# Retention in a two-block transformer kernel: weight sums by adding transfers, sums of x through PSUM, and one operation for normalising and gating

## The reference, cut to what matters

```
q, k, v, g = split(h @ w_in)              # h = rmsnorm(x); w_in is 1024 x 6144
q, k = rope(q), rope(k) * 256 ** -0.5
...                                       # state and decay in chunks of 64
o = o_intra + o_cross                     # (512, 4 heads, 512)
mu, var = mean(o), mean((o - mu) ** 2)    # over the 512 of a head
o = (o - mu) * rsqrt(var + EPS) * gn_g
y = silu(g) * o
x = x + y @ w_out
```

## Time and profile before

| | us |
|---|---|
| median of 3 runs | 1906.8 (1903.63 to 1907.77) |
| profiled execution, device time | 1903.31 |
| its span in the trace | 1901.5 |
| mean granted clock of TensorE | 0.988 of full |
| TensorE busy | 1830.7 |
| VectorE, ScalarE, GpSimd busy | 1262.2, 874.0, 1018.6 |
| retention, from the spread of the first norm to the end of head 3 | about 545 to 985 |

### The profile page before, as it was taken

One profiled execution on the slowest core, in us unless ns is written; L12 is line 12 of the kernel. 1 busy time (PEld: TensorE's weight loads), 2 busy tenths in 40 slices (PEclk: granted clock), 3 DMA queues, 4 the chain that ended last, 5 costly groups with the idle time before them and its releaser, 6 DMA issues.

```text
span 1901.5 us, 23957 instructions
## 1 busy us (share of the span) xinstructions
PE 1830.7 (96%) x9348; PEld 1557.2 (82%) x9348; DVE 1262.2 (66%) x1908; ACT 874.0 (46%) x1350; POOL 1018.6 (54%) x431
## 2 busy tenths in 40 slices
PE   9999999999977999999899999999999999999998
PEld 7778889898865787878689898988888887888886
DVE  6986875776779667575766354457777766454546
ACT  5345443343543424243446444454666655453444
POOL 5573465475535365656438475665333335664755
PEclk9999999999997999999999999999999999999999
DMA  5222414423245325151342422312433223414221
GB/s 183 89 89 77 145 67 148 159 92 106 80 147 183 133 71 187 66 171 67 110 145 77 133 89 89 134 45 66 121 109 101 88 69 109 155 47 149 92 90 55
DMA packets 143344, 206.02 MB, mean 108 GB/s; under 512 B 4320, under 2 KB 94704, under 8 KB 142720
## 3 DMA queue, kind: packets, MB, share of 16 engines
q1 hardware_dynamic: 135968, 192.16, 30.2%
q10 hardware_dynamic: 7264, 12.34, 2.2%
HBM read 193.96 MB, written 10.53 MB: 108 GB/s over the span
## 4 chain that ended last, share of the span: by engine, by line
PE 72%; DVE 15%; ACT 4%; issue 3%; POOL 1%; DMA 0%; ACTq 0%; DVEq 0%
PE ps L858 23%; PE ps L860 23%; PE ps L859 23%; DVE ps L2315 1%; POOL w_lo L824 1%; ACT w_hi L1411 1%; DVE w_lo L2563 1%; DVE work L2611 1%; DVE raw L2549 1%; DVE diagonals L1983 1%; DVE work L2778 1%; DVE work L2574 0%; DVE probs_t_lo L2797 0%; PE ps L1198 0%; DVE x L2627 0%
## 5 line engine op out<-in xcount | busy, mean ns | idle before, releaser
L824 POOL TENSOR_TENSOR w_lo<-raw,w_hi 128x1024 fp32r<-128x1024 f32 x216 | 527.4, 2451 | 609.4 <-ACT w_hi L1411 609.4
L858 PE MATMUL ps<-xh,w_hi 128*128 128x512 f32 x1280 | 504.9, 394 | 4.6 <-DVE xl L2009 2.3
L860 PE MATMUL ps<-xh,w_lo 128*128 128x512 f32 x1280 | 498.9, 390 | 0.0
L859 PE MATMUL ps<-xl,w_hi 128*128 128x512 f32 x1280 | 498.8, 390 | 0.0
L1411 ACT ACTIVATE w_hi<-raw 128x1024 fp32r<-128x1024 f32 x242 | 252.2, 1057 | 392.9 <-PE ps L860 344.2
L858 PEld LDWEIGHTS ps<-xh,w_hi 128*128 128x128 f32 x1280 | 240.7, 188 | 58.5 <-issue 8.9
L859 PEld LDWEIGHTS ps<-xl,w_hi 128*128 128x128 f32 x1280 | 240.8, 188 | 50.7 <-issue 1.9
L860 PEld LDWEIGHTS ps<-xh,w_lo 128*128 128x128 f32 x1280 | 240.7, 188 | 50.7
L858 PE MATMUL ps<-hid,w_hi 128*128 128x256 f32 (+1 forms) x688 | 228.4, 332 | 2.1 <-DVE att_v L2751 1.1
L860 PE MATMUL ps<-hid,w_lo 128*128 128x256 f32 (+1 forms) x688 | 227.1, 330 | 0.0
L859 PE MATMUL ps<-hid,w_hi 128*128 128x256 f32 (+1 forms) x688 | 227.0, 330 | 0.0
(11 more groups left out here) (302 smaller groups left out, 3546.7 us busy)
## 6 DMA issues: line engine op xcount, KB each, us to landing
raw<-in_mlp_w_dram SPq DMA_DIRECT2D x40, 1024.0 KB, 5.5
work<-in_mlp_w_dram SPq DMA_DIRECT2D x16, 1024.0 KB, 5.5
raw<-in_ret_w_in_dram SPq DMA_DIRECT2D x12, 1024.0 KB, 5.2
raw<-in_att_w_in_dram SPq DMA_DIRECT2D x12, 1024.0 KB, 5.3
raw<-in_w_gate_dram SPq DMA_DIRECT2D x11, 1024.0 KB, 5.4
raw<-in_w_up_dram SPq DMA_DIRECT2D x11, 1024.0 KB, 5.5
hid<-position_sums SPq DMA_DIRECT2D x10, 1024.0 KB, 5.2
raw<-in_w_in_dram SPq DMA_DIRECT2D x9, 1024.0 KB, 5.1
```

The source lines that it names most:

```text
L824: nc.gpsimd.tensor_tensor(half_of(wl[:, b % 2, :], b, half), half_of(source, b, half), half_of(wh[:, b % 2, :], b, half).bitcast(F32), ALU ...
L858: nc.tensor.matmul(o, a[0], b[0], start=first, stop=False, skip_group_check=True)
L859: nc.tensor.matmul(o, a[0], b[1], start=False, stop=False, skip_group_check=True)
L860: return nc.tensor.matmul(o, a[1], b[0], start=False, stop=last, skip_group_check=True)
```

## The change

- `d2` and `d4` leave `BY_VECTOR`: GpSimd makes their low halves too.
- The four sums of quarters are made by transfers that add into the holder. GpSimd issues them: `b12` gets `b11` added (behind the `k` block, for `d1`), then `b22` (behind `d1`'s low halves, for `d2`), then `b21` (behind `d2`'s, for `d4`); `b22` gets `b12` added (behind `h22`'s low halves, for `d3`). Differences become sums, with signs moved to the sums of x and to `value_sum`. Each of the 16 transfers moves 1 MB.
- The order in which SyncE fetches changes; `h22`'s sum of x stays in SBUF and is no longer stored and fetched; the stores have a semaphore each.
- Sums of x: a first sum `w` is built in PSUM, the others from it, with ScalarE scaling tiles into PSUM; all five steps stand before the diagonals, the last two behind `rope` of the queries.
- TensorE in head 0: `h11` ahead of `spread`, scores behind `h22`. Last head: the mix of tiles 2 and 3 behind `h21`, as in the other heads.
- `refine_root` in four operations instead of five, its first value in PSUM. `normalised` goes: ScalarE scales the gates by the root's inverse (`scale_gate`), and `gated` subtracts the mean and multiplies in one operation.
- `scale_x` moves: tiles 0 to 3 ahead of `gate_sum`, tiles 4 to 7 ahead of the output sums.

The diff, cut to its core:

```
-BY_VECTOR = ("t2", "t4", "d2", "d4")
+BY_VECTOR = ("t2", "t4")
...
+            def add_to(held, name, h, signal):
+                dst = holders[holder_of(held, h)].rearrange("p (k c) -> p k c", c=512)
+                nc.gpsimd.dma_start(dst, head_weights(name, h), accum_op=ALU.add).then_inc(signal, 16)
...
-                if kind == "h11":
...
-                    for cut in (slice(0, 1024), slice(1024, 2048)):
-                        nc.gpsimd.tensor_tensor(first[:, cut], second[:, cut], first[:, cut], ALU.subtract).then_inc(d1_made, 1)
+                if kind == "own" and own_at[b][0] == "k":
+                    h = own_at[b][1]
+                    pool.wait_ge(*landed("b12", h))
+                    add_to("b12", "b11", h, p1_landed)
+                if kind == "d1":
                     pool.wait_ge(w_lo, lows[2 * b + 2])
+                    add_to("b12", "b22", head_of(b), p2_landed)
                 if kind == "h22":
...
+                    pool.wait_ge(w_lo, lows[2 * b + 2])
+                    add_to("b22", "b12", head_of(b), p3_landed)
+                if kind == "d2":
+                    pool.wait_ge(w_lo, lows[2 * b + 2])
+                    add_to("b12", "b21", head_of(b), p4_landed)
...
+                    def scale_gate(h):
+                        act.wait_ge(root_refined, h + 2)
+                        for s in range(ST):
+                            act.wait_ge(gate_made, 4 * h + s + 1)
+                            nc.scalar.activation(sg[:, s, :], sg[:, s, :], ACT.Copy, scale=t4[:, s:s + 1]).then_inc(gate_scaled, c.made(gate_scaled))
...
                     for h in range(RET_HEADS):
                         head_quarter("h11", h)
-                        head_scores()
-                        for kind in ("d1", "h22", "d2", "d3"):
-                            head_quarter(kind, h)
+                        if h == 0:
+                            spread()
+                        else:
+                            head_scores()
+                        head_quarter("d1", h)
+                        head_quarter("h22", h)
+                        if h == 0:
+                            head_scores()
+                        head_quarter("d2", h)
+                        head_quarter("d3", h)
...
                     def gated(i):
-                        dve.wait_ge(gate_made, c.next(gate_made))
-                        dve.wait_ge(dve_step, c.now(dve_step))
-                        V.tensor_tensor(o_sb[:, i, :], o_sb[:, i, :], sg[:, i, :], ALU.mult).then_inc(p_ready, c.made(p_ready))
+                        dve.wait_ge(gate_scaled, c.next(gate_scaled))
+                        V.scalar_tensor_tensor(o_sb[:, i, :], o_sb[:, i, :], mv[:, i, 0:1], sg[:, i, :],
+                                               ALU.subtract, ALU.mult).then_inc(p_ready, c.made(p_ready))
...
-                        second_difference(h)
-                        difference_lo("d2", h)
-                        fourth_difference(h)
-                        if h == 0:
-                            scale_x(range(0, 4))
...
+                        if h == 0:
+                            scale_x(range(0, 4))
+                        gate_sum(0)
+                        gate_sum(1)
+                        mixed_stats()
+                        gate_copy(0)
+                        refine_root()
+                        gate_copy(1)
+                        for i in range(ST):
+                            gated(i)
...
-                    position_sum(0)
-                    position_sum(1)
-                    position_sum_lo(0)
-                    position_sum_lo(1)
+                    for kind in ("w", "d2", "d1"):
+                        position_sum(kind)
+                    position_sum_lo("d1")
+                    position_sum_lo("d2")
                     rope(qh, ql, 0)
+                    position_sum("h22")
+                    position_sum_lo("h22")
+                    position_sum("d3")
+                    position_sum_lo("d3")
                     V.tensor_copy(ms, r1c).then_inc(to_curve, c.made(to_curve))
                     refine_root()
                     diagonals(rc2, spread=False)
-                    position_sum(2)
-                    position_sum(3)
-                    position_sum_lo(2)
-                    position_sum_lo(3)
                     rope(kh, kl, 2, take_r1=True)
```

More of the change, by code:

```diff
@@ L393, in build @@
         sum_lo = sem("sum_lo")
-        sums_stored = sem("sums_stored")
+        sum_stored = [sem(f"sum_stored{i}") for i in range(4)]
         sum_landed = [sem(f"sum_landed{i}") for i in range(3)]
@@ L480, in head_source @@
                 return holders[holder_of(*own_at[b])]
-            return holders[roles[head_of(b)][{"h11": 0, "d1": 0, "h22": 2, "d2": 0, "d3": 1, "h21": 3, "d4": 0}[plan[b]]]]
+            return holders[roles[head_of(b)][{"h11": 2, "d1": 0, "h22": 1, "d2": 0, "d3": 1, "h21": 3, "d4": 0}[plan[b]]]]
         def first_turn(f):
@@ L618, in _ @@
                     sp.wait_ge(unit_done, 2 * (begins("ffn") + 30))
[L619 removed]
                     fetch("b12", 0)
+                    fetch("b22", 0)
                     for h in range(RET_HEADS):
@@ L1202, in _ @@
                     first_units(order, double=True)
-                    spread()
                     for h in range(RET_HEADS):
@@ L2502, in refine_root @@
-                        V.tensor_tensor(rc2, rc2, ms2, ALU.mult).then_inc(dve_step, c.made(dve_step))
-                        dve.wait_ge(dve_step, c.now(dve_step))
-                    def position_sum(n):
-                        u, s1, s2, s3 = (by_tile(sum_rows[m]) for m in (2, 0, 1, 2))
-                        s4 = by_tile(sum_rows[3])
-                        if n == 0:
+                        V.scalar_tensor_tensor(rc2, ms2, 1.5, root_guess, ALU.add, ALU.mult).then_inc(root_refined, c.made(root_refined))
@@ L2510, in position_sum @@
+                    def position_sum(kind):
+                        near, far, held = slice(0, 256), slice(256, 512), by_tile(ps[:, 6:8, :])
+                        if kind == "w":
                             dve.wait_ge(scaled_x, 4)
+                        elif kind == "d3":
+                            dve.wait_ge(scaled_x, 8)
                         else:
                             dve.wait_ge(sum_made, c.now(sum_made))
+                        k0, cut, op = {"w": (0, near, ALU.add), "d2": (0, far, ALU.subtract), "d1": (0, near, ALU.add),
+                                       "h22": (4, near, ALU.add), "d3": (0, near, ALU.subtract)}[kind]
+                        made = held if kind == "w" else by_tile(sum_rows[SUM_ROW[kind]])
@@ L2513, in position_sum @@
                         for k in range(4):
-                            g, g_beyond = prow("mix_norm_g_2", k), prow("mix_norm_g_2", 4 + k)
-                            near, far = (slice(0, 256), slice(256, 512))
-                            out_, in_, scale, op, other = ((s1, x[:, 4 + k, far], g_beyond, ALU.add, u), (s2, x[:, k, near], g, ALU.subtract, s1),
-                                                           (s3, x[:, k, near], g, ALU.subtract, u), (s4, x[:, 4 + k, near], g_beyond, ALU.add, s2))[n]
@@ L2518, in position_sum, with position_sum_lo @@
-                            V.scalar_tensor_tensor(out_[:, k, :], in_, scale, other[:, k, :], ALU.mult, op).then_inc(sum_made, c.made(sum_made))
-                    def position_sum_lo(n):
+                            V.scalar_tensor_tensor(made[:, k, :], x[:, k0 + k, cut], prow("mix_norm_g_2", k0 + k), held[:, k, :], ALU.mult, op).then_inc(
+                                sum_made, c.made(sum_made))
+                    def position_sum_lo(kind):
+                        n = SUM_ROW[kind]
                         dve.wait_ge(sum_hi, c.next(sum_hi))
-                        dve.wait_ge(sum_made, 4 * (n + 1))
+                        dve.wait_ge(sum_made, sums_upto[kind])
@@ L2655, in head @@
                         value_lo(1)
-                        if h == 0:
-                            scale_x(range(4, KT))
-                            dve.wait_ge(dve_step, c.now(dve_step))
                         value_sum(2)
```

243 lines of the change are left out of this document (102 added, 141 removed).

## The result

The changed kernel takes 1895.27 us in the median of four runs (1893.47 to 1896.8), the kernel before 1906.86 beside it. The ratio is 0.9942, with a 95% interval of 0.9925 to 0.9959: 11.6 us faster, where 17.9 were forecast. The profiled execution took 1893.47, its span is 1891.5.

What follows compares the result with a forecast made beforehand. TensorE, busy 96%, bounds the kernel; only its waits (48 us for VectorE) and lower clock can pay. Head 0 12.6, heads 1 and 2 8.4, head 3 2.2, start 0, transfers -6: 17.2 us off, forecast 1889, range 1879 to 1908.

Steps and rivals of the forecast that it cites:

- the 12.6 of head 0: Head 0's gain: 9.2 us value-sum wait, 1.9 us gated-tiles wait and 1.5 us of lower clock all go.
- signs named for being right: No kept-product or value-sum wait over 1 us, no 9 us head-0 wait; named head times, landings and last-transposes wait.
- those for being wrong: `w_lo` waits over 4 us for `d2` or `d3`, ScalarE idle for DMA, issues over 2.5, start stillness past 22.
- VectorE's part in heads 1 to 3: Eight passes a head go, saving waits of 1.5 + 0.8 us a head, and 1.1 more in head 3.
- Gates in heads 0 to 2: Last gate done by 748.5 or 750.9 us, before TensorE's transposes at 751.2, so 1.9 us goes in each head.
- The last head: Head 3's gate chain: table load, four scalings and two gates replace two contended gates; a loss of 1.2 us.
- The start: Before and into head 0: `h11` fills 5.5 of 13.0 us, diagonals come later; 0 taken, between -4 and +4.
- The transfers in heads 1 to 3: Adding transfers at 9 us and issues at 1 cost 2 us a head, 6 in all, between nothing and 45.
- The two deadlines of 10.2 and 9.9 us: Time in a head for transfer 2 to land for `d2` and transfer 3 for `d3`; 9 us just fits both.
- The held issue: Rival: GpSimd's transfer issues held 2 to 3 us by VectorE, 3 us more a head, 1898 us; chance 0.14.
- Gain in head 0: 9.2, and 1.5 of clock: Moving `scale_x` from ahead of head 0's kept product removes the 9.2 us wait and 1.5 us of lower clock.
- Head 0 ... nothing: Transfers cost head 0 nothing: low halves of `d1` and `h22` are early, a score block more precedes `d2`.

Runs made afterwards that it cites:

- experiment 7: Changed kernel with masked scores kept in PSUM, plus transfer 3 split into two of 512 KB with a semaphore each: 1879.77 us, ratio 0.9865.
- experiment 6: Changed kernel with scores kept in PSUM, plus the last head's order from before the change (scalings split accordingly): 1885.26 us, ratio 0.9902.
- experiment 10: Changed kernel, scores in PSUM, their high halves earlier, transfer 3 halved, last head's gate curves and scalings ahead of two conversions: 1875.01 us, ratio 0.9841.
- experiment 2: Changed kernel with GpSimd's transfers as plain copies without adding, so its output is not the stage's: 1877.29 us, ratio 0.9852.
- experiment 8: Kernel before the change, with only scale_x moved and the scores kept in PSUM: 1895.50 us, ratio 0.9949.
- experiment 1: Changed kernel with the masked scores left in their PSUM bank instead of SBUF: 1883.52 us, ratio 0.9884.
- experiment 5: Changed kernel with head 0's score high halves two units earlier on ScalarE, ahead of the conversion waiting for transfer 3: 1882.74 us, ratio 0.9879.

## Why the prediction was right, and where it was not

The sign was right, and the time, 1895.27 us, lies in the range, at the far end of the 1885 to 1896 that the forecast gave to its own case. But 11.6 us were gained instead of 17.9, and the sum is not made up as forecast: its largest term, the 12.6 of head 0, came to next to nothing, and 5.0 us that it did not have (3.7 at the start, 1.3 in heads 1 to 3) made up for a part of that. That the sum held so far is luck. Of the signs named for being right three came (heads 1 and 2 at 95 to 98 us, transfers 2 and 3 landing in 8.3 to 10.8, the last transposes waiting 8.6) and two did not: value sums are waited for by more than 1 us, and a 9 us wait stands in head 0. One of those for being wrong came, ScalarE idle for a DMA (6.63 us). By steps:

**VectorE's part in heads 1 to 3: right, but for the value sums of heads 2 and 3.** The kept product's 1.5 us a head and the value sum's 0.8 in head 1 are gone. In heads 2 and 3 value sums of 1.2 and 1.4 us stand, more than the 0.8 that were to go; they too go with a shorter transfer 3 (experiment 7). Heads 1 and 2 take 95.7 and 96.5 us, in the 95 to 98 named. All three heads together gained 5.9 where 4.6 were forecast.

**Gates in heads 0 to 2: right.** The transposes there wait for nothing: the list has one wait at L1204 instead of four. The operation on 128 x 4 that took 2.42 us is gone, and the four of `refine_root` take 0.16 to 0.19 each.

**The last head: right in size, not in its terms.** 8 to 9 us were forecast and 8.6 stand there, 1.2 more than the 7.4 of the earlier trace rows. The chain shows whose they are:

```profile
928.48 0.70 ACT w_hi L1420
...
929.44 1.04 ACT w_hi L1420
...
930.50 1.28 ACT L1711
...
931.80 1.33 ACT work L1711 x2
933.13 0.62 ACT work L1718
...
933.77 3.04 DVE work L2615 x4
```

Two conversions for the output product come first in ScalarE's order, then the table load (1.28, the row without a tile), curves, a scaling, four gates at 0.76. I had counted four scalings there (2.7 us) and two gates behind them; one scaling and four gates stand. The old order (experiment 6), which takes the table load, two scalings and two gates off this path, shortened the wait by 1.0 and the run not at all, so the terms of that sum are not borne out. I had left out the conversions, since they stood there before too; experiment 10 shows that they, with the table load that then no longer waits behind them, were worth 3.3 us.

**The start: right within its bounds.** TensorE waits 7.8 us for the diagonals instead of 13.0, and no longer for the keys (4.7 before). But a wait of 4.9 stands ahead of `h11` that I did not have:

```profile
562.26 0.79 PE L867 MATMUL ps<-w_hi,xh 128*128 128x512 f32 x1 [4.91 <-DVE work L2505]
```

L2505 is the last of the four reads in `rope` that free the two PSUM banks of the queries, and `h11` needs one of them. In VectorE's order they stand behind the sums of x and their low halves. So `h11` does not simply fill 5.5 of the 13.0 us. The diagonals came sooner than the 579.5 that I had:

```profile
577.05 0.69 DVE L2002 TENSOR_TENSOR diagonals<-ident,cols 128x512 f32<-128x512 f32 x1
...
584.57 1.23 DVE L2515 TENSOR_TENSOR k_parts<-work,k_parts 128x1024 fp32r<-128x1024 f32 x1 [0.53 <-ACT k_parts L1438]
```

TensorE spreads them and is in `d1` at 580.19; before, it was in the scores at 583.92. With equal products left at both points that is 3.7 us sooner, close to the good bound of 4. Both kernels then pay for the stillness with the lower clock; in the changed one:

```profile
580.19 0.80 PE L867 MATMUL ps<-w_hi,hid 128*128 128x512 f32 x1 [0.32 <-DVE work L2505]
```

The first seven products take 3.16 us (the eighth starts at 583.35), 0.43 apart after the first one, where 1.6 would do. The kernel before starts its scores with a row of 0.79 in the same way. So the start gave about the 3.7, and the rest of the first window, head 0, next to nothing: there the waits are 9.4 + 0.6 + 0.7 = 10.7 us where 9.2 + 1.9 = 11.1 were.

**The transfers in heads 1 to 3: right.** Assumed were 9 us to landing and 1 on GpSimd. The DMA view, 535 to 990 us (KB, median us from issue to landing), of the changed kernel (`work` is transfer 3; the other two mix transfers 1, 2 and 4):

```profile
holder<-in_ret_w_in_dram POOLq DMA_DIRECT2D x6, 1024.0 KB, 8.5
raw<-in_ret_w_in_dram POOLq DMA_DIRECT2D x6, 1024.0 KB, 8.7
...
work<-in_ret_w_in_dram POOLq DMA_DIRECT2D x4, 1024.0 KB, 10.0
```

and of experiment 2, without the adding:

```profile
holder<-in_ret_w_in_dram POOLq DMA_DIRECT2D x6, 1024.0 KB, 6.4
...
raw<-in_ret_w_in_dram POOLq DMA_DIRECT2D x6, 1024.0 KB, 6.0
...
work<-in_ret_w_in_dram POOLq DMA_DIRECT2D x4, 1024.0 KB, 5.4
```

Transfer 3 sits on the chain in each of heads 1 to 3, for 9.57, 10.48 and 10.77 us; in head 1 the chain reads:

```profile
690.94 1.29 POOL raw L785
692.22 4.79 POOL w_lo L833 x2
697.01 0.29 issue
697.30 9.57 DMA work<-in_ret_w_in_dram
706.98 1.07 ACT w_hi L1420
708.13 4.76 POOL w_lo L833 x2
712.93 0.51 PE ps L867
```

`d3` starts when its low half is made, with 0.68 us of wait in head 1. The sum was 6 us for the three heads; experiment 2 gives 6.6 back, and with the scores in PSUM 7.5 (295.8 to 288.3 us from head 1's scores on). The two deadlines of 10.2 and 9.9 us were the right thing to compare with: transfer 2 landed in 8.4 to 8.7 us, transfer 3 in 9.1 to 10.8. The Trainium skill (Collectives: The Full Stack, "The bandwidth ceiling: the fold count and why AG ≠ RS ≠ AR") has, for reductions between cores, the add free and the rate halved by the second read. The trace agrees with the direction, 8.5 to 10.0 us against 5.4 to 6.4, but in duration from issue to landing that is a factor of 1.3 to 1.9.

**The held issue: wrong.** The 15 issues of adding transfers on GpSimd from 582 us on take 1.28 to 1.32 us each, also beside VectorE's work; none was held. The contention was there, but it held VectorE, and on a part that no rival named.

**The step that failed: head 0.** It read "Gain in head 0: 9.2, and 1.5 of clock", and of the transfers "Head 0 ... nothing". The first half held for the edit alone: moving `scale_x` in the kernel before gave 11.2 us by the medians. The second half did not hold. I had checked that the weights come in time for TensorE, and they do: no wait for `w_lo` in head 0 is over 0.7 us. I had not looked at what stands behind the waiting conversion in ScalarE's order. Before, the scores came ahead of `d1`, and ScalarE made their high halves without a landing to wait for. The change moves the scores of head 0 behind `h22`, and their high halves behind `d3`'s conversion, which now waits for a landing. So they start 3 us late, and with them VectorE's low halves, which run into 10 us of unbroken subtractions on GpSimd; the kept product and the value sum stand behind those. Under the same subtractions `scale_x` had taken its 8.96 us before (experiment 8); I had taken that time as found, and not asked what made it so long. The term is 9.4 us of wait and 1.9 of lower clock, and three different edits take most or all of it out again: an operand moved to PSUM (-9.5 in head 0), a transfer that lands 3.4 us sooner (-9.5), and an order in which the scores don't wait for it (head 1's scores start at 678.8 instead of 689.9, -11.1). Against the sum: 17.2, less the 12.6 of head 0, plus 3.7 at the start (together the 3.8 of the first window, to 0.1) and 1.3 more in heads 1 to 3, is 9.6; measured are 10.0 between the spans.

The Trainium skill has the rule for the port (SBUF — State Buffer, "Who interferes with whom"): a VectorE operation with two SBUF inputs contends with a GpSimd operation that reads SBUF, one with a single SBUF input does not. The trace agrees, 8.99 us with two and 1.68 with one, under the same GpSimd passes (experiment 1), and 1.69 with two and GpSimd idle (experiment 5). I had used that page only for the issues.

**Not tried.** An order of the start with the diagonals ahead of the sums of x. Transfer 1 took 10.7 to 12.6 us to land, longer than the others, and why is not known; it has the time, so nothing waits for it. No run takes the start's 3.7 us or the relief of heads 1 to 3 by itself: these are read from the two traces.

## What to carry to other kernels

When a wait on one engine's ordered queue becomes a wait for a transfer, it is not enough that the data come in time for their own reader: list what stands behind the wait in that queue, and who waits for those, up to the engine that bounds the kernel. A VectorE step that reads two SBUF tiles should not be allowed to slide into a stretch of GpSimd passes; here one operand in PSUM was enough to make it safe. And when a short operation shows a long duration, ask what ran beside it before moving it away: what comes to stand in its place may pay the same. Try the cheap move by itself, too: moving `scale_x` gave as much as the whole change (1894.61 against 1895.27), because the new wait had eaten the rest; with that wait cured by order alone the change took 1882.74. And the gains of experiments that cure the same wait do not add up.

## What the runs showed of the hardware

- A transfer from GpSimd that adds 1 MB from DRAM into SBUF lands 8.5 to 10.0 us after its issue (medians by holder; single ones 8.3 to 12.6), a plain one from the same queue in 5.4 to 6.4. The issue takes GpSimd's time too: 1.3 us for an adding one, 0.77 for a plain one.
- Four small VectorE subtractions (128 rows, 512 to 128 wide) take 1.69 us with GpSimd idle, 8.99 while GpSimd subtracts without a break, and 1.68 with one input in PSUM under the same passes. Four of `scale_x` (128 x 512, two inputs in SBUF) take 8.96 us under such passes and 2.49 behind them.
- Two 512 KB adding transfers, issued one behind the other, take 7.4 us each to land, and 2.42 us of GpSimd for the two issues.
